# A hybrid convolution and attention step: who makes the low part of the gated output, and what TensorE does until the first x is there

## What is computed

```
def conv_mixer(x, prefix, g_norm, w_in, w_dw, b_dw, ln_g, ln_b, w_out):
    h = rms_norm(x, g_norm)
    u = jnp.einsum('btd,de->bte', h, w_in)
    a, gl, z = jnp.split(u, 3, axis=-1)
    v = a * jax.nn.sigmoid(gl)
    ...
def band_attention(q, k_ctx, v_ctx, key_valid, sinks):
    s = jnp.einsum('bqkgd,bskd->bkgqs', qg, k_ctx,
    ...
    m = jnp.maximum(jnp.max(s, axis=-1, keepdims=True), sink)
    p = jnp.exp(s - m)
    denom = jnp.sum(p, axis=-1, keepdims=True) + jnp.exp(sink - m)
    p = (p / denom).astype(v_ctx.dtype)
    o = jnp.einsum('bkgqs,bskd->bqkgd', p, v_ctx)
    return o.reshape(b, tq, D_ATTN)
...
def attn_output(x, o, z, w_out):
    return x + jnp.einsum('bte,ed->btd', o * jax.nn.silu(z), w_out)
```

## Time and profile before

| | |
|---|---|
| median of 3 runs | 1705.86 us (1705.12 to 1711.52) |
| the profiled execution: time | 1704.73 us |
| its span, first to last instruction | 1702.9 us |
| what lies around the span | 1.8 us |
| PE, PEld busy | 97%, 79% |
| DVE, ACT, POOL busy | 75%, 46%, 38% |

### The profile page before, as it was taken

How to read it: one execution, slowest core, us unless ns; L and a number is a source line. 1 busy time by engine, 2 the same in 40 slices (tenths; PEclk the granted TensorE clock), 3 DMA queues, 4 the chain that set the end, 5 groups by cost and what they waited for, 6 DMA issues and landing times.

```text
span 1702.9 us, 26944 instructions
## 1 busy us (share of the span) xinstructions
PE 1644.7 (97%) x10267; PEld 1349.6 (79%) x10267; DVE 1272.8 (75%) x1944; ACT 778.9 (46%) x1625; POOL 648.8 (38%) x504
## 2 busy tenths in 40 slices
PE   7999999999999988999999999978999999999998
PEld 6899888888898876888888888756777777777776
DVE  6479889898888657889889433567777777777774
ACT  6655555565554545443343333454333443333431
POOL 2489999999985304445444332200000000000000
PEclk9999999999999999999999999989999999999999
DMA  7411111121120555444454342744222233322311
GB/s 218 129 58 43 50 48 55 48 69 44 62 89 28 181 195 201 139 158 156 156 149 156 119 155 80 234 146 129 97 97 72 85 106 115 103 102 91 104 62 44
DMA packets 153722, 186.06 MB, mean 109 GB/s; under 512 B 51028, under 2 KB 116668, under 8 KB 149450
## 3 DMA queue, kind: packets, MB, share of 16 engines
q1 hardware_dynamic: 149274, 172.54, 31.8%
q10 hardware_dynamic: 4320, 11.80, 1.8%
HBM read 116.41 MB, written 70.72 MB: 110 GB/s over the span
## 4 chain that ended last, share of the span: by engine, by line
PE 60%; POOL 22%; DVE 7%; ACT 3%; DMA 3%; issue 3%; SPq 1%; POOLq 0%; DVEq 0%; ACTq 0%
POOL a_csum L489 21%; PE c_acc L121 19%; PE b_pso L121 15%; PE b_psq L121 9%; PE c_pso L2357 4%; PE a_ps L741 3%; DVE a_pst L639 3%; PE c_pss L2334 2%; PE c_psp L2342 2%; POOL a_csum L486 1%; PE b_pst L1510 1%; PE a_pst L705 1%; PE c_pso L2351 1%; DVE w L109 1%; PE c_pst L2258 1%
## 5 line engine op out<-in xcount | busy, mean ns | idle before, releaser
L741 PE MATMUL a_ps<-a_xt,a_wring 128*128 128x512 f32 (+3 forms) x2880 | 557.7, 354 | 9.5 <-ACT a_zo L551 6.4
L741 PEld LDWEIGHTS a_ps<-a_xt,a_wring 128*128 128x128 f32 x2880 | 495.0, 189 | 65.8 <-ACT a_zo L551 8.0
L489 POOL TENSOR_TENSOR a_csum<-a_prod,a_csum 128x704 f32<-128x704 f32 (+1 forms) x231 | 405.3, 1754 | 43.1 <-ACT a_prod L538 9.9
L639 DVE SCALAR_TENSOR_TENSOR a_pst<-a_vbuf,taps,a_pst 128x704 f32<-128x704 f32 (+1 forms) x338 | 314.1, 929 | 10.4
L538 ACT ACTIVATE a_prod<-a_vbuf,taps 128x704 f32<-128x704 f32 (+1 forms) x252 | 214.7, 863 | 166.5 <-POOL a_csum L489 154.9
L121 PE MATMUL c_acc<-w,c_ht 128*128 128x512 f32 x768 | 184.8, 396 | 3.0 <-DVE c_sz L2019 2.3
L121 PE MATMUL b_pso<-w,b_yt 128*128 128x512 f32 x768 | 182.2, 393 | 0.7 <-DVE b_yt L1312 0.7
L121 PEld LDWEIGHTS c_acc<-w,c_ht 128*128 128x128 f32 x768 | 142.8, 189 | 39.2 <-issue 10.3
L121 PEld LDWEIGHTS b_pso<-w,b_yt 128*128 128x128 f32 x768 | 141.9, 188 | 29.5 <-DVE b_yt L1312 1.1
L1886 ACT ACTIVATE c_es<-c_es 128x4 f32<-128x4 f32 x64 | 13.1, 205 | 198.4 <-DVE c_es L2044 198.4
L121 PE MATMUL b_psq<-b_w,b_ht 128*128 128x512 f32 x384 | 94.9, 403 | 4.5 <-DVE b_w L109 4.5
(11 more groups left out here) (247 smaller groups left out, 2242.3 us busy)
## 6 DMA issues: line engine op xcount, KB each, us to landing
ht_d<-b_ht SPq DMA_DIRECT2D x16, 1024.0 KB, 5.0
c_ht<-ht_d SPq DMA_DIRECT2D x16, 1024.0 KB, 5.0
a_stage<-in_w_in_a SPq DMA_DIRECT2D x24, 512.0 KB, 4.2
a_x<-in_x_prompt SPq DMA_DIRECT2D x16, 512.0 KB, 3.6
b_cz<-c_d SPq DMA_DIRECT2D x16, 512.0 KB, 5.6
b_cz<-z_d SPq DMA_DIRECT2D x16, 512.0 KB, 4.1
b_x<-in_x_prompt SPq DMA_DIRECT2D x16, 512.0 KB, 4.2
x_d<-b_x SPq DMA_DIRECT2D x16, 512.0 KB, 2.6
```

The lines of the kernel that those rows point to most:

```text
L489: pool.tensor_tensor(out, prod[:, (PTAPS * n + i) % RING, 0:t1 - t0], out, ALU.add).then_inc(prod_added, 1)
L639: dve.scalar_tensor_tensor(part if k == DTAPS - 1 and not last else here, vbuf[:, b % 2, t0 + k:t1 + k], wcol(k, b), part if k == 0 else h ...
L741: last = pe.matmul(out, wring[:, u % 3, a, k], xt[c][:, e, k, 0:n], start=(k == 0 and a == 0 and e == 0), stop=(k == KT - 1 and a == 1))
```

## The change

Three things are changed. (1) In phase C, the low part of the gated output is made by GpSimd (`pool.tensor_tensor`, the same subtraction) for tiles 0 to 14; tile 15 stays on DVE. (2) In phase A, TensorE multiplies a constant by itself into a PSUM bank that is not in use yet: 22 times before the first transpose, 2 times after tile 0's transposes and 7 times ahead of the first group of products. The constant is made one place later on POOL and the semaphore's count moved with it. (3) SP loads x(1) ahead of the gain.

```
@@ sync, phase A
             load_x(0)
+            load_x(1)
             sp.dma_start(gain[:, :], io.norm_a.rearrange("(a d) -> a d", a=1).broadcast_to([P, D])).then_inc(gain_in, 16)
-            load_x(1)
             load_unit(0)
@@ gpsimd, phase A
-            pool.memset(g.share[:, :], 1.0 / D)
-            pool.memset(g.ln_eps[:, :], LN_EPS).then_inc(ident_made, 1)
+            pool.memset(g.ln_eps[:, :], LN_EPS)
+            pool.memset(g.share[:, :], 1.0 / D).then_inc(ident_made, 1)
@@ tensor, phase A
+            def warm(n):
+
+                ones = g.share[:, :].broadcast_to([P, P])
+                for _ in range(n):
+                    pe.matmul(bank[3][:, 0:P], ones, ones, start=True, stop=True)
+
+            pe.wait_ge(ident_made, 2)
+            warm(22)
             pe.wait_ge(ident_made, 4)
...
                     if plan.turn_at[t] == 2 * i:
                         turn_x(t)
+                        if t == 0:
+                            warm(2)
+                if i == 0:
+                    warm(7)
@@ vector, phase C
             scores(G, t, 0, 0, r)
             if first:
                 prev.last_fold()
-            else:
-                cut_o(t - 1)
             gate(t, 0)
@@ phase C
+    def gpsimd(pool):
+        prev.gpsimd(pool)
+        for t in range(TILES - 1):
+            pool.wait_ge(ohi_ready, t + 1)
+            pool.tensor_tensor(ot[:, 1], szc[:, :, :], f32(ot[:, 0]), ALU.subtract).then_inc(olo_ready, 1)
+
...
-    p.sync, p.gpsimd, p.scalar, p.vector, p.tensor = sync, prev.gpsimd, scalar, vector, tensor
+    p.sync, p.gpsimd, p.scalar, p.vector, p.tensor = sync, gpsimd, scalar, vector, tensor
```

## The result

The changed kernel takes 1720.52 us (median of 7 runs, 1716.76 to 1722.40) against 1703.55 us (7 runs on the same chip): 17.0 us more, a ratio of 1.009 with a 95% interval from 1.0076 to 1.0103. A ratio here is worked out over all the runs and isn't the quotient of the two medians, from which it can differ by 0.001. The changed kernel's profiled execution took 1718.26 us, 13.5 us more than that of before.

The account below looks back on a forecast made before the run. TensorE was taken to set phase C's pace, waiting on the chain of scores, exponentials, tanh and gate. 1704.73 + 19.2 (subtraction on POOL) - 1.0 (start) = 1722.9, predicted as 1723 us, range 1711 to 1731.

Parts of the forecast that it names:

- Part 1: Phase C: taking the subtraction off DVE frees 18.3 us of DVE time, nothing of the span; wait grows 1.82 to 3.04.
- Part 2, POOL's duration and the standing: Phase C: POOL's subtraction takes 2.44 us; DVE's two-SBUF-operand maximum of head 0 stands until it ends, then needs 0.55 us.
- rival of mere sharing: Phase C maximum: engines only share bandwidth, costing 0.2 us a tile, 3 us in all; chance 0.14 together with no standing.
- DVE could come first: Phase C: maximum precedes POOL, a later small DVE instruction stands instead; 18 us minus start, 1722; 0.78 together with main case.
- Part 2, what a tile loses: Phase C: later z(t, 1) costs 1.26 us in eleven tiles, 0.88 to 1.49 in the others; sum 19.2 us.
- term of 1.26 us: Phase C, tile 8: maximum 1.76 us late less 0.5 of play; tanh, gate and z(t, 1) are 1.26 us late.
- the play: Phase C: about 0.5 us by which the chain from DVE's scores to z(t, 1) can slip, ScalarE being idle before tanh.
- Part 3, the start: Phase A's start: constants and earlier x(1) gain 1.0 us; bounds a loss of 1.2 and a gain of 2.3.
- both the first group's earlier start and its pace reach the later groups: Phase A's start: condition for the upper bound, a gain of 2.3 us from earlier start (1.2) and pace (1.1).
- The sum: Whole kernel: 1704.73 + 19.2 - 1.0 = 1722.9 us, predicted as 1723; bounds of the terms 1719.5 to 1728.1.
- half made good: Phase C, behind z(t, 1): TensorE's slack takes half the delay, leaving 9.6 us, 1713.3 us in all; chance 0.06.

Follow-up runs that it names:

- late subtraction: Changed kernel with POOL's subtraction also waiting until DVE's last small instruction of head 0's scores is done; 1709.66 us, ratio 1.0019 to the kernel before.
- kernel with quarters: Changed kernel with POOL's subtraction cut into four instructions of 256 columns; 1712.32 us, ratio 1.0031 to the kernel before.
- half subtraction: Changed kernel with POOL making 512 columns of the low part early and DVE the other 512 in its old place; 1708.75 us, ratio 1.0011.

## Why the prediction was right, and where it was off

The forecast was 1723 us and slower; 1720.52 is inside its range, and the mechanism is the one named. That the sum came so near is in part luck: tiles 2 to 15 were put 3.2 us too high and the start 1.0 us or more too low, and the two errors offset each other.

- **Part 1**, nothing to gain from DVE's free time: right. The gate stands behind 2.37 us of idle DVE, and TensorE waits for it. (The wait grew less than to 3.04 us, since DVE came to it later.)
- **Part 2, POOL's duration and the standing**: right. 2.397 us for 2.44, the maximum 2.43 for 2.45, 1.57 in tile 1 (1153.01 - 1151.44 = 1.57), 2.71 in tile 3 (2.68), 2.16 in tile 15 (2.18). The rival of mere sharing falls on the maximum's end behind POOL's in two widths and on the late subtraction. That DVE could come first did not happen in any tile; in the kernel with quarters it did, and POOL's second quarter stood.
- **Part 2, what a tile loses**: the mechanism right, the term of 1.26 us too large. In tile 8 the maximum is 1.74 us late against `z(t, 0)` and the tanh 1.17, so the play there is 0.57 us, not 0.5. Then `z(t, 1)` comes 8.36 us after `z(t, 0)`, for 7.31 before: 1.05. Most of the missing 0.12 us lay on TensorE itself: before, it began `z(t, 1)` 0.24 us after the gate's end, behind its other work, and now 0.14 after. The half subtraction says the same: 0.63 us late costs these tiles nothing. By the distances of the gates, tiles 7 to 14 lose 0.99 us each, tiles 4 and 6 1.13 and 1.14, tiles 3 and 5 1.45 and 1.39 (1.49), tile 15 1.46 (1.49). Tile 2 loses 0.57, and tile 1's own `z(1, 1)` is 0.87 us late, as predicted (0.88); waits for loads follow at these two, and differ by up to 2 us from execution to execution, so that what remains of them can't be told. Tiles 2 to 15 add up to 15.1 us, where the prediction had 18.3; tiles 3 to 15, free of those loads, to 14.5, where it had 17.0.
- **Part 3, the start**: the term failed, a gain of 1.0 us that came out as none (0.2 us behind at the second gate, 0.2 ahead at the last), or rather as a small loss: with the five other executions of this start, the second gate is at 44.02 to 45.19 us and phase A's last at 553.31 to 554.27, against 43.51 and 43.77, 552.89 and 553.49 in the two executions with the old start. The step "both the first group's earlier start and its pace reach the later groups" was weighed by the first group alone. What was late next was x(3), and the pause ahead of it cost the pace that the constants had bought. Three kernels show it: with x(3) moved up, without the swap, and with both, the lead stays through phase A.
- **The sum**: +15.1 in tiles 2 to 15, and the profiled execution reached tile 1's gate 1.6 us earlier, nearly all of it between phases B and C. That is spread: one and the same kernel came to tile 1's gate at 1157.42 and 1155.01 us in two executions, and the six executions with this start to tile 0's gate, ahead of anything in which they differ, at 1109.92 to 1114.38. The rival "half made good" is refuted: the play was in the term already, and nothing behind `z(t, 1)` gave more back.

## What to carry to other kernels

Before work goes from DVE to an idle GpSimd, look at which DVE instructions will run beside it: here those with two operands in SBUF stood until a GpSimd instruction that reads had ended, and where they lie on the chain to TensorE, the whole delay is paid, less the play. If the work must go there, start it behind those instructions and end it ahead of whoever overwrites its input (the late subtraction failed the second, at 3.5 us in all), or keep the lock about as short as the play (the half, 1.2 us); splitting it into four took away two thirds of the loss and left 4.8 us. And of work that warms an engine up: ask what is late next, since a pause right behind it can lose the pace again.

## What the runs showed that was not expected

Instructions on 128x4 are held like large ones: 0.56 and 0.66 us for 0.16, when a 256-column subtraction on POOL ran beside them. Four subtractions of 256 columns, with DVE's work between, take POOL 3.27 us where one of 1024 takes 2.40, since POOL stands behind DVE's maximum as DVE stands behind POOL. Writing 1024 columns of zeros takes POOL 0.95 us and holds up nobody. And TensorE's granted clock read 0.50 after a pause of 2.45 us at the start (stretch 22 to 24 us), and so in all six executions with this start, while pauses of 0.35 and 1.29 us there left the pace as it was. In the kernel before, the column reads 1.00 while twelve products took 2.90 us at 15.68, so at the very start it doesn't show the pace:

```profile
16.00:18.00 2.00, 2.00 (x11) 2.00 (x11) 1.76 (x2) 2.00 (x4) 0.76 (x3) 1.00 0.95 334
```
